# Attention of a transformer block: heads in pairs, PE transposes, row sums divided out on GpSimd, V parts side by side, outputs kept on chip

## The reference, cut to what matters

```python
qn_l, qr_l = mla_queries(q_cl, q_norm, w_q_up)      # per head 64 + 32 columns
kn_l, v_l = mla_kv(kv_cl, kv_norm, w_kv_up)         # per head 64 + 64
kn_c, v_c = mla_kv(kv_cc, kv_norm, w_kv_up)
qr_l = apply_rope(qr_l, cos[:, None], sin[:, None])
kr_l = apply_rope(kr_l, cos, sin)                   # one rotary key for all heads
...
s = jnp.einsum('bqhd,bkhd->bhqk', qn, k_nope) + jnp.einsum('bqhr,bkr->bhqk', qr, k_rope)
p = jax.nn.softmax(s.astype(F32) * MLA_SCALE, axis=-1)
return jnp.einsum('bhqk,bkhd->bqhd', p.astype(v.dtype), v)
...
out_lat = o_l.reshape(B, L, MLA_HEADS * MLA_V) @ w_out
```

## Time and profile before

| | us |
|---|---|
| median of three runs | 3472.11 |
| the profiled execution: its span (the page gives no other time of it) | 3480.0 |
| attention, from the first scores to the last output | 353.7 |
| TensorE busy in it | 324.0 |
| TensorE idle between the last output and the output projection | 17.9 |

### The profile page before, as it was taken

One profiled execution on the slowest core, in us unless ns is written; L12 is line 12 of the kernel. 1 busy time (PEld: TensorE's weight loads), 2 busy tenths in 40 slices (PEclk: granted clock), 3 DMA queues, 4 the chain that ended last, 5 costly groups with the idle time before them and its releaser, 6 DMA issues.

```text
span 3480.0 us, 43974 instructions
## 1 busy us (share of the span) xinstructions
PE 3165.0 (91%) x17179; PEld 2579.0 (74%) x17179; DVE 1605.2 (46%) x2431; ACT 830.3 (24%) x1251; POOL 232.6 (7%) x383
## 2 busy tenths in 40 slices
PE   5699999999976989999998999999879998789997
PEld 2288888887843768787886888888658887567785
DVE  4143334446456353333336444344646666255444
ACT  0311111114253131111113211111434444142212
POOL 0100000000010000000000000000013332000000
PEclk7699999999988999999999999999999999899999
DMA  4543332211121233433320222221110000222331
GB/s 150 180 131 126 127 119 62 72 37 49 48 75 52 73 101 105 139 114 130 123 73 25 85 60 60 60 67 54 29 41 22 20 21 23 86 85 87 94 96 37
DMA packets 296206, 273.13 MB, mean 78 GB/s; under 512 B 31735, under 2 KB 259935, under 8 KB 296000
## 3 DMA queue, kind: packets, MB, share of 16 engines
q1 hardware_dynamic: 270944, 190.78, 18.3%
q0 software_dynamic: 21760, 76.03, 6.2%
q10 hardware_dynamic: 3424, 5.25, 0.5%
HBM read 264.68 MB, written 7.34 MB: 78 GB/s over the span
## 4 chain that ended last, share of the span: by engine, by line
PE 80%; DVE 7%; DMA 5%; ACT 5%; issue 2%; SPq 0%; POOL 0%; POOLq 0%; ACTq 0%; DVEq 0%
PE PSALL L1836 24%; PE PSALL L1837 23%; PE PSALL L1838 23%; DMA ADA<-in_ada_w_dram 4%; PE PSALL L2152 2%; PE PSALL L1930 1%; ACT H L779 1%; PE PSALL L1790 1%; PE PSALL L1807 1%; ACT HHI L782 1%; PE PSALL L2042 1%; DVE RSTD L1382 1%; ACT SQ L861 1%; DVE X L1387 1%; PE PSALL L1937 1%
## 5 line engine op out<-in xcount | busy, mean ns | idle before, releaser
L1836 PE MATMUL PSALL<-HHI,WHIA 128*128 128x512 f32 (+1 forms) x1552 | 550.0, 354 | 85.7 <-DVE WLOA L1282 39.4
L1837 PE MATMUL PSALL<-HLO,WHIA 128*128 128x512 f32 (+1 forms) x1552 | 542.8, 350 | 0.0
L1838 PE MATMUL PSALL<-HHI,WLOA 128*128 128x512 f32 (+1 forms) x1552 | 541.8, 349 | 0.0
L1836 PE MATMUL PSALL<-HHI,WHIB 128*128 128x512 f32 (+1 forms) x1520 | 524.8, 345 | 8.2 <-DVE WLOB L1282 8.2
L1320 DVE SCALAR_TENSOR_TENSOR X<-PSALL,GATE,X 128x512 f32<-128x512 f32 (+1 forms) x616 | 377.8, 634 | 328.8 <-PE PSALL L1838 327.5
L1837 PE MATMUL PSALL<-HLO,WHIB 128*128 128x512 f32 (+1 forms) x1520 | 524.6, 345 | 0.0
L1838 PE MATMUL PSALL<-HHI,WLOB 128*128 128x512 f32 (+1 forms) x1520 | 523.8, 345 | 0.0
L1836 PEld LDWEIGHTS PSALL<-HHI,WHIA 128*128 128x128 f32 x1552 | 298.4, 192 | 145.1 <-DVE WLOA L1282 40.1
L1838 PEld LDWEIGHTS PSALL<-HHI,WLOA 128*128 128x128 f32 x1552 | 298.8, 192 | 37.4
L1837 PEld LDWEIGHTS PSALL<-HLO,WHIA 128*128 128x128 f32 x1552 | 299.6, 193 | 34.3
L1836 PEld LDWEIGHTS PSALL<-HHI,WHIB 128*128 128x128 f32 x1520 | 288.0, 189 | 43.9 <-issue 8.6
(11 more groups left out here) (255 smaller groups left out, 4450.5 us busy)
## 6 DMA issues: line engine op xcount, KB each, us to landing
RAW<-in_ffn_w_in_dram SPq DMA_DIRECT2D x176, 512.0 KB, 4.3
ADA<-in_ada_w_dram POOLq DMA_DIRECT2D x144, 512.0 KB, 5.5
RAW<-in_ffn_w_out_dram SPq DMA_DIRECT2D x88, 512.0 KB, 3.7
RAW<-in_ev_w_in_dram SPq DMA_DIRECT2D x20, 512.0 KB, 4.4
WRAW<-in_mla_w_q_up_dram SPq DMA_DIRECT2D x16, 288.0 KB, 2.8
RAW<-in_ev_w_out_dram SPq DMA_DIRECT2D x8, 512.0 KB, 4.7
...
```

What stands on the lines that cost most here:

```text
L1836: te.matmul(out, w_hi, x_hi(k), start=(k == 0), stop=False)
L1837: te.matmul(out, w_hi, x_lo(k), start=False, stop=False)
L1838: x = te.matmul(out, w_lo, x_hi(k), start=False, stop=(k == ks - 1))
```

## The change

- **Turns.** The transposes are real transposes with the identity, `te.transpose`. The division by the row's sum is done ahead of them, on GpSimd, in place on PR (`normalise`, one per part). DIAG is gone.
- **Keys.** The keys of two heads are made in one group of products (128 columns of weights). ScalarE takes them out of PSUM to K32, makes the high part (`keys_high`), and GpSimd the low part (`keys_low`). A head of even number has its keys on rows 0 to 63, one of odd number on rows 64 to 127. The rotary key stands twice in the other half, and the queries carry the cosine and the sine part in it, so no sum is needed in the rotation: one multiplication of 128 x 512 (`rotate`) takes the place of three operations and a copy. Scores run over 128 rows.
- **V.** The high and the low part of a head's V lie side by side (VALL), so one weight of 128 columns serves both: 12 products per two parts instead of 18. The upper half of the result is V's low part's share; ScalarE copies it out (`out_low`) and VectorE adds the two (`out_sum`) into O32. With it the product low x low is formed too. GpSimd's copies of V are gone.
- **Outputs** stay on chip: O32, split by pair to OHI (ScalarE) and OLO (GpSimd); the store, the load and OCH are gone, and the projection reads OHI and OLO. The first projection weights are split during the last pair.
- **Weights.** ScalarE makes the main high parts of the query weights (`weights_main`), GpSimd the swapped ones and the low parts.
- **Order.** The loops over pairs are written out. On ScalarE the copy to PTH of g-1 stands ahead of the exponential of g, on VectorE PTL of g-1 ahead of the reciprocal of g.

```diff
@@ -115,7 +115,8 @@
     ang = np.stack([(t // GRID_W)[None, :] * inv[:, None], (t % GRID_W)[None, :] * inv[:, None]])
     cos = np.repeat(np.cos(ang)[:, None], 2, 1).reshape(ROPE, LAT)
     sin = np.stack([-np.sin(ang), np.sin(ang)], 1).reshape(ROPE, LAT)
-    out["rope"] = np.concatenate([cos, sin, cos, sin])
+    ones = np.ones((NOPE, LAT))
+    out["rope"] = np.stack([np.concatenate([ones, cos, sin]), np.concatenate([cos, sin, ones])])
     return {k: np.ascontiguousarray(v, dtype=np.float32) for k, v in out.items()}
...
-    VH, VL = (place(f"V{n}", [P, TB, MH * VD], F32R) for n in "HL")
...
+    VALL = sb("VALL", [P, PAIRS, 2, TB, 2, VD], F32R, at=h_at)
+    OHI = [sb(f"OHI{i}", [P, LAT], F32R, at=h_at + 6144 * i) for i in range(PAIRS)]
+    OLO = [sb(f"OLO{i}", [P, LAT], F32R, at=h_at + 6144 * i + 2048) for i in range(PAIRS)]
...
-    OD = nc.dram_tensor("heads_out", (MH * VD, LAT), F32, kind="Internal").ap()
...
-            sp.wait_ge(o_out[z], 16 * MH)
-        for m in range(KC):
-            sp.dma_start(OCH[:, m, :], OD[m * P:(m + 1) * P, :]).then_inc(och_in, 16)
...
-        def head_weights(i, d):
...
-        def head_values(z, h):
...
+        def key_weights(i):
+            pool.wait_ge(wk_in, 32 * (i + 1))
+            if i >= 1:
+                pool.wait_ge(k_pe, 2 * i)
+            raw = WKRAW[:, :, :, :].rearrange("p k z n -> p k (z n)")
+            same(WKH[:, :, :], raw).then_inc(wk_hi, 1)
+            pool.wait_ge(wk_hi, i + 1)
...
+        def normalise(g):
+            pool.wait_ge(s_inv, g + 1)
+            pool.tensor_scalar(PR[g % 2][:, :], PR[g % 2][:, :], STAT[g % 2][:, 3:4], None, ALU.mult).then_inc(s_norm, 1)
...
+        for i in range(PAIRS):
+            more = i + 1 < PAIRS
+            g = 8 * i
+            normalise(g)
+            pool.wait_ge(s_norm, g + 1)
+            keys_low(2 * i + 1)
+            pool.wait_ge(k_lo, 2 * i + 2)
+            normalise(g + 1)
+            if more:
+                key_weights(i + 1)
+                weights_swapped(2 * i + 2)
+            queries(2 * i + 1)
+            normalise(g + 2)
+            normalise(g + 3)
+            if more:
+                weights_low(2 * i + 2)
+            normalise(g + 4)
+            if i:
+                heads_low(i - 1)
+            normalise(g + 5)
+            if more:
+                keys_low(2 * i + 2)
+                queries(2 * i + 2)
+            normalise(g + 6)
+            if more:
+                weights_swapped(2 * i + 3)
+            normalise(g + 7)
+            if more:
+                weights_low(2 * i + 3)
+        heads_low(PAIRS - 1)
...
-            act.wait_ge(och_in, 16 * KC)
-            act.wait_ge(av_pe, 2 * MH)
-            for m in range(KC):
-                act.activation(HHI[:, m, 0:LAT], OCH[:, m, :], ACT.Copy).then_inc(och_hi, 1)
...
+            def out_low(e):
+                act.wait_ge(av_pe, e + 1)
+                if e >= 2:
+                    act.wait_ge(o_add, e - 1)
+                act.activation(TMPO[e % 2][:, :], PS[6][VD:P, CTX * (e % 2):CTX * (e % 2) + CTX], ACT.Copy).then_inc(o_tmp, 1)
+            def heads_high(i):
+                act.wait_ge(o_add, 4 * i + 4)
+                act.activation(OHI[i][:, :], O32[i][:, :], ACT.Copy).then_inc(och_hi, 1)
...
+                    if s % 2 and g >= 5:
+                        out_low((g - 5) // 2)
+                    if more and s in (3, 4):
+                        keys_take(i + 1, s - 3)
+                    if g:
+                        turned(g - 1)
+                    probs(g)
+                    if s == 0:
+                        keys_high(2 * i + 1)
+                    if s == 4 and i:
+                        heads_high(i - 1)
+                    if more:
+                        if s == 1:
+                            weights_main(2 * i + 2)
+                        if s == 5:
+                            keys_high(2 * i + 2)
+                        if s == 6:
+                            weights_main(2 * i + 3)
+                    elif s == 5:
+                        act.wait_ge(q_pe, MH)
+                        for half in range(2):
+                            split_hi("A", half, b.q + half, 0, b.A)
+            turned(8 * PAIRS - 1)
+            for e in (4 * PAIRS - 2, 4 * PAIRS - 1):
...
+            def rotate(h):
+                dve.wait_ge(q_pe, h + 1)
+                if h >= 2:
+                    dve.wait_ge(q_lo, h - 1)
+                dve.tensor_tensor(QT[h % 2][:, :], PS[7][:, :], ROT[h % 2][:, :], ALU.mult).then_inc(q_rot, 1)
...
+            def out_sum(e):
+                h = e // 2
+                rows, cols = slice(VD * (h % 2), VD * (h % 2) + VD), slice(CTX * (e % 2), CTX * (e % 2) + CTX)
+                dve.wait_ge(o_tmp, e + 1)
+                dve.tensor_tensor(O32[h // 2][rows, cols], PS[6][0:VD, cols], TMPO[e % 2][:, :], ALU.add).then_inc(o_add, 1)
...
+                    if g:
+                        turned(g - 1)
                     dve.wait_ge(s_exp, g + 1)
                     dve.reciprocal(st[:, 3:4], st[:, 2:3]).then_inc(s_inv, 1)
-                    dve.wait_ge(s_inv, g + 1)
-                    dve.tensor_scalar(DIAG[s % 2][:, :], ID[:, :], st[:, 3:4], None, ALU.mult).then_inc(s_norm, 1)
-                    if not (first and s == 0):
-                        turned(i, s - 1)
...
-                    x = te.matmul(TR_[:, t, :], PR[s % 2][:, t * P:(t + 1) * P], DIAG[s % 2][:, :], start=True, stop=True)
+                    x = te.transpose(TR_[:, t, :], PR[g % 2][:, t * P:(t + 1) * P], ID[:, :])
...
-                product(PS[6][0:VD, 0:CTX], [(VSH[z][:, t, :], VSL[z][:, t, :]) for t in range(TB)], None,
-                        lambda t: PTH[half][:, t, :], lambda t: PTL[half][:, t, :]).then_inc(av_pe, 1)
...
+                out = PS[6][:, CTX * (e % 2):CTX * (e % 2) + CTX]
+                for n, part in enumerate((PTH[e % 2], PTL[e % 2])):
+                    for t in range(TB):
+                        x = te.matmul(out, VALL[:, h // 2, h % 2, t, :, :].rearrange("p a n -> p (a n)"), part[:, t, :],
+                                      start=(n == 0 and t == 0), stop=(n == 1 and t == TB - 1))
+                x.then_inc(av_pe, 1)
...
+            for i in range(PAIRS):
+                more = i + 1 < PAIRS
+                for s in range(8):
+                    g = 8 * i + s
+                    if s in (1, 2):
+                        query_part(2 * i + 1, s - 1)
+                    if more and s in (3, 4):
+                        key_part(i + 1, s - 3)
+                    if more and s in (5, 6):
+                        query_part(2 * i + 2, s - 5)
+                    scores(g)
+                    if g:
+                        turn(g - 1)
+                    if s % 2 == 0 and g >= 4:
+                        outputs(g // 2 - 2)
+            turn(8 * PAIRS - 1)
+            for e in (4 * PAIRS - 2, 4 * PAIRS - 1):
+                outputs(e)
...
-            project("mla_out", 1, 2, kk, lambda k, s: te.wait_ge(och_lo, k + 1), evac, 2)
...
+            project("mla_out", 1, 2, kk, lambda k, s: te.wait_ge(och_lo, k + 1), evac, 2, (OHI, OLO))
```

453 lines of the change are left out of this document (216 added, 237 removed).

## The result

Before 3470.72 us, after 3479.72 us (medians of 18 runs each on one chip); the ratio is 1.0026, 95% interval 1.0018 to 1.0035. The forecast was 3394.5, range 3368 to 3434. The profiled executions have spans of 3480.0 and 3480.4 us, so the two traces can be laid side by side.

What follows compares the result with a forecast made beforehand. It took TensorE, busy for 91% of the 3480.0 us span, to bound the kernel. The terms -55.5 + 5 - 27.1 = -77.6 us gave a span of 3402.4, less 7.9 a time of 3394.5, range 3368 to 3434.

Steps and rivals of the forecast that it cites:

- X: GpSimd's multiplication of a 128x768 tile by the sums' reciprocals, ahead of each turn; taken as 0.85 us.
- The bounds themselves: Limits for the length of GpSimd's multiplication: 0.75 us from a memset, 1.85 us from reading two tiles.
- the prediction's slope: About 48 us of time for each us that GpSimd's multiplication takes longer.
- the 298.2 of the forecast: Forecast time from first scores to last output, 298.2 us over eight pairs of heads, against 353.7 before.
- The clock: Thinner TensorE work would lower the clock for one turn in each of seven pairs: 5 us, between 0 and 45.
- The second rival: The clock falls in every step with a wait: 22 to 55 us, time 3412 to 3444; chance 0.13.
- TensorE's work: TensorE's sum from first scores to last output: 14.8 us per head, 237 in all, 87 us less work.
- The chain: From turn to turn: transposes, PTH copy, exponential, reciprocal and handovers, 3.15 us, plus GpSimd's multiplication, 4.0 us in all.
- Behind the stage: At the output projection, the 17.9 us wait goes and the first 48 products take 10.9 instead of 20.1: 27.1 us.
- Ahead of it: Before the first scores: 2.4 us of added KRT copies less 3.4, counted as 0, between -3 and +3.
- The fourth rival: GpSimd's multiplication holds the turn so long that the gain goes: 3480 at 2.6 us; chance 0.03.
- The prediction's own signs: Signs of being wrong: pairs under 33 us, GpSimd's multiplication over 1.2 us, or the stage's clock under 0.9.

Runs made afterwards that it cites:

- e2: Changed kernel with GpSimd's normalisation as a TENSOR_TENSOR that reads the column of reciprocals over and over: 3430.73 us, ratio 0.9886.
- e7: Changed kernel with 12 unused TensorE products of 256 columns in three of eight steps, to hold the clock up: 3456.22 us, ratio 0.9957.
- e10: Changed kernel with the normalisation on VectorE in two halves of 384 columns, the first releasing three transposes: 3367.87 us, ratio 0.969.
- e9: Changed kernel with the normalisation shared, 256 columns on GpSimd and 512 on VectorE: 3416.27 us, ratio 0.9822.
- e11: Changed kernel with the normalisation on ScalarE instead of GpSimd: 3391.99 us, ratio 0.9757.
- e6: Changed kernel without any normalisation, the turn waiting for the reciprocal alone: 3358.92 us, ratio 0.9683.
- e1: Changed kernel with the normalisation on VectorE behind the reciprocal instead of on GpSimd: 3370.77 us, ratio 0.971.
- e5: Changed kernel with GpSimd multiplying by the constant 0.5 instead of the column of reciprocals: 3473.44 us, ratio 1.0008.

## Why the prediction was wrong, point by point

**The failing step is X, "I take 0.85, from the row that reads one tile".** It measured 2.20 to 2.23 us. I had bounded it by 0.75 and 1.85 and chosen the one row out of line with the rest, an operation of another kind on 128 columns. The zero-adding rows, which the prediction counts as reading two operands, read one tile and a single column over and over; by them X would be 1.46, and e2, which does just that as a multiplication, measured 1.48. The bounds themselves came from instructions of other kinds, because the trace before held no TENSOR_SCALAR on GpSimd; "two tiles read" was no upper end for it. By the prediction's slope, 48 x (2.20 - 0.85) = 65 us of the 88. e7, where the clock is up, bears that out: with its last outputs its stage takes some 362 us, 64 more than the 298.2 of the forecast. How the time follows X, over the kernels of this order (e10, with its two instructions, apart; the times of e9 and e11 come from the chip where the kernel before took 5 us longer):

| where, how | X, us | stage, us | its clock | time, us |
|---|---|---|---|---|
| none (e6) | 0 | 253.3 | 0.99 | 3358.9 |
| VectorE (e1) | 0.73 | 271.7 | 0.98 | 3370.8 |
| ScalarE (e11) | 0.94 | 288.7 | 0.96 | 3392.0 |
| GpSimd, 256 columns (e9) | 1.18 | 312.7 | 0.94 | 3416.3 |
| GpSimd, TENSOR_TENSOR (e2) | 1.48 | 330.6 | 0.90 | 3430.7 |
| GpSimd, constant (e5) | 2.14 | 374.8 | 0.89 | 3473.4 |
| GpSimd, as changed | 2.23 | 382.8 | 0.88 | 3479.7 |

The stage grows by 58 us for each us of X from e9 to e2, and by 69 from e2 to the changed kernel. The falling clock is in both; the forecast's 48 leaves it out.

The Trainium skill (GPSIMD Engine Reference, Performance versus the Vector engine) gives 1.03 cycles an element for a body bound by its read and write ports and about 2.6 for the two inputs of `tensor_tensor`; at the page's 1.2 GHz an estimate is 0.86 and 2.17 ns. The subtractions of the earlier trace rows agree with the second, at 2.17 ns. The products here do not follow the pair: TENSOR_SCALAR, with one tile, costs 2.5 ns a column, and TENSOR_TENSOR 1.68. The page's advice beside it, to do elementwise work on VectorE, is what e1 bears out.

**The clock, "I put 5 us for it".** e7 puts it at 24, within the bounds of 0 to 45, and 65 + 24 = 89 agrees with the 88 that were missing. The 5 us had counted one half-clock turn a pair for waits of 1.6 to 2.3 us; with X at 2.20 the longest waits of the steps are 3 us and over. The second rival had the mechanism, but as something apart from X, where it is its consequence. The Trainium skill's rule that the high clock does not engage for transposes (TensorE: Matmul & The Clock Gate, PE-mode transpose) was rightly put aside: a turn behind a wait of 2.97 took 0.87 us at a granted clock of 1.00.

**TensorE's work, 237 us,** is right (238.3 in e1).

**The chain "3.15 plus X"** is right link by link: for X = 2.20 it gives 5.35 and 5.16 was measured, the handovers being shorter by that much. By its slope X of 0.73 and 0.94 would make 3389 and 3399; e1 and e11 came in 18 and 7 us below that. On these engines no key and weight work of GpSimd stands ahead of the normalisation, which the forecast had charged for. The trace of e1 shows it: the two steps of a pair that were charged take 4.48 and 4.30 us there (fourth pair), where the forecast's rule gives 5.2 and 5.0 with X = 0.73. Over eight pairs that is 11 of the 18 us; the rest is not accounted for.

**Behind the stage, -27.1:** measured -29.6. The kernels e1 to e11, which share the code there, have 487.5 to 490.6 us behind the stage, 26.6 to 29.7 less than before, so the term was right. **Ahead of it, 0:** measured -2.6, within its 3; but with the same code ahead the stage began anywhere from 2602.2 to 2617.1 us in these traces, so one pair of traces can't tell.

**The fourth rival** came true in its size (about 3480), at X = 2.2 instead of 2.5, since the clock added its 24 us; I gave it 0.03. The prediction's own signs, a GpSimd row over 1.2 us and a stage clock under 0.9, are both there.
